# Rolling the PE and SP expert steps of a mixture-of-experts decoder layer into hardware loops

## The reference, cut to what matters

```python
logits = (x @ w_router + b_router).astype(jnp.float32)
top_logit, top_idx = lax.top_k(logits, TOP_K)            # TOP_K = 4 of N_EXPERTS = 32
top_w = jax.nn.softmax(top_logit, axis=-1)
...
def expert_block(args):
    xk, e = args
    a = xk @ w_up[e] + b_up[e]                           # D = 1024 -> 2 * 1024
    a_glu = jnp.minimum(a[:, :D_EXPERT], SWIGLU_LIMIT)
    a_lin = jnp.clip(a[:, D_EXPERT:], -SWIGLU_LIMIT, SWIGLU_LIMIT)
    o = a_glu * jax.nn.sigmoid(SWIGLU_ALPHA * a_glu) * (a_lin + 1)
    return o @ w_down[e] + b_down[e]                     # 1024 -> 1024
```

## Time and profile before

| | |
|---|---|
| median of three runs | 1538.55 us (1538.19 to 1539.16) |
| the profiled execution | 1538.55 us, span from first to last instruction 1536.5 us |
| PE busy | 1407.7 us (92% of the span), 9490 matmuls |
| DVE, ACT, POOL busy | 515.4, 272.5, 24.3 us |
| mean granted TensorE clock | 0.976 of full speed |
| read from HBM | 452.54 MB, 296 GB/s over the span |

### The profile page before, as it was taken

One profiled execution on the slowest core, in us unless ns is written; L12 is line 12 of the kernel. 1 busy time (PEld: TensorE's weight loads), 2 busy tenths in 40 slices (PEclk: granted clock), 3 DMA queues, 4 the chain that ended last, 5 costly groups with the idle time before them and its releaser, 6 DMA issues.

```text
span 1536.5 us, 23462 instructions
## 1 busy us (share of the span) xinstructions
PE 1407.7 (92%) x9490; PEld 859.0 (56%) x9490; DVE 515.4 (34%) x1339; ACT 272.5 (18%) x454; POOL 24.3 (2%) x43
## 2 busy tenths in 40 slices
PE   5699897799999999999999999999999999999996
PEld 4577675544455554545555555555555455555554
DVE  2279633311233322313332234333232232234333
ACT  1111201201121111101121211112221111211113
POOL 1021000000000000000000000000000000000000
PEclk9899998699999999999999999999999999999998
DMA  9933767146599995877999999999999689999930
GB/s 301 360 138 110 271 242 280 46 154 215 203 341 378 380 333 203 318 273 274 365 378 370 378 377 378 380 379 378 368 381 351 231 315 359 381 378 378 377 116 32
DMA packets 225543, 456.01 MB, mean 297 GB/s; under 512 B 4992, under 2 KB 5624, under 8 KB 225365
## 3 DMA queue, kind: packets, MB, share of 16 engines
q1 hardware_dynamic: 225050, 452.74, 81.2%
q0 software_dynamic: 160, 1.00, 0.2%
q10 hardware_dynamic: 203, 0.22, 0.0%
HBM read 452.54 MB, written 2.01 MB: 296 GB/s over the span
## 4 chain that ended last, share of the span: by engine, by line
PE 73%; ACT 5%; issue 3%; DVE 2%; DVEq 0%; ACTq 0%
PE ps L1138 51%; PE ps L1112 8%; PE ps L1192 7%; PE ps L1144 4%; ACT ufull L546 2%; ACT sq L528 1%; ACT sq L550 1%; PE ps L1223 1%; DVE uv L869 1%; PE ps L1093 1%; PE ps L1062 1%; PE ps L948 0%; PE ps L1259 0%; DVE hT L897 0%; PE ps L1070 0%
## 5 line engine op out<-in xcount | busy, mean ns | idle before, releaser
L1138 PE MATMUL ps<-ring,sq 128*64 128x256 f32 (+1 forms) x2848 | 398.3, 397 | 25.5 <-ACT sq L550 25.5
L1138 PEld LDWEIGHTS ps<-ring,sq 128*64 128x64 f32 (+1 forms) x2848 | 226.9, 141 | 177.7 <-issue 88.1
L843 DVE TENSOR_SCALAR sg<-ps 128x512 f32<-128x512 f32 x64 | 44.3, 692 | 538.9 <-PE ps L1144 538.9
L1138 PE MATMUL ps<-ring,ufull 128*64 128x256 f32 (+1 forms) x1408 | 198.5, 400 | 12.2 <-ACT ufull L546 12.2
L1138 PEld LDWEIGHTS ps<-ring,ufull 128*64 128x64 f32 (+1 forms) x1408 | 114.1, 142 | 90.0 <-issue 28.7
L542 ACT ACTIVATE pbuf<-sg 128x512 f32<-128x512 f32 x64 | 40.3, 630 | 558.3 <-DVE sg L843 558.3
L1112 PE MATMUL ps<-rows,ufull 128*64 128x256 f32 (+1 forms) x732 | 121.5, 412 | 5.2 <-issue 5.2
L846 DVE TENSOR_SCALAR wpool<-ps 128x512 f32<-128x512 f32 x64 | 44.3, 692 | 242.8 <-PE ps L1144 242.8
L1192 PE MATMUL ps<-ufull,sq 64*128 64x288 f32 (+1 forms) x528 | 122.6, 443 | 3.3 <-ACT sq L550 1.6
L986 PE MATMUL ps<-hT,ring 128*128 128x288 f32 x448 | 112.5, 413 | 10.9 <-DVE hT L643 9.2
L869 DVE TENSOR_TENSOR uv<-uv,ps 128x288 f32<-128x288 f32 x264 | 107.3, 451 | 19.7 <-PE ps L1192 12.4
(11 more groups left out here) (199 smaller groups left out, 968.0 us busy)
## 6 DMA issues: line engine op xcount, KB each, us to landing
ring<-in_w_up_dram SPq DMA_DIRECT2D x96, 2048.0 KB, 11.1
ring<-in_w_down_dram SPq DMA_DIRECT2D x48, 2048.0 KB, 10.7
pbuf<-in_w_up_dram SPq DMA_DIRECT2D x16, 2048.0 KB, 9.0
sg<-in_w_up_dram SPq DMA_DIRECT2D x16, 2048.0 KB, 11.4
ring<-in_w_ada_dram SPq DMA_DIRECT2D x12, 2048.0 KB, 10.4
pbuf<-in_w_down_dram SPq DMA_DIRECT2D x8, 2048.0 KB, 10.2
sg<-in_w_down_dram SPq DMA_DIRECT2D x8, 2048.0 KB, 11.7
ring<-in_w_in_dram SPq DMA_DIRECT2D x7, 2048.0 KB, 20.1
```

The lines of the kernel that those rows point to most:

```text
L843: V.tensor_scalar(glu, ps[:, UP_BANKS[2 * h], :], LIMIT, None, ALU.min)\
L1138: ins = pe.matmul(ps[a * width:(a + 1) * width, UP_BANKS[j], 0:cols], tokens(k), w[:, k, a * cols:(a + 1) * cols], start=(k == 0), stop=(k ...
```

## The change

Two Python loops over the eight groups of four experts become hardware loops: SP's in `expert_weights` and PE's in the pass that always runs. PE's stream then holds the code of four experts once, and at its end a branch back to its beginning; the step number is a register. So the values of the semaphore waits in it (`2 * n + 1`, `KT * g + 7`, `turn * 16 + ...`) are computed into registers by instructions of the engine's sequencer, the three token counts are loaded from an address that depends on a register (`bass.ds(e + i, 1)`), and SP's DMAs take a source address from a register. What is computed, the order of the work, the tiles and the waits stay.

```diff
             sp.wait_ge(m_ready, KT)
-            for step in range(NE // UNROLL):
+            with sp.Fori(0, NE // UNROLL) as step:
                 expert_weights(0, step)
...
                 sized(first, lambda width: (gather(width), turn_gathered(p * GAT, width)))
-                def four_experts(step):
+                with pe.Fori(0, NE // UNROLL) as step:
                     turn = p * (NE * EXPERT_CHUNKS // NRING) + step * TURNS
                     for u in range(UNROLL):
                         e = step * UNROLL + u
...
-                            last, this, nxt = (pe.value_load(cnti[0:1, e + i:e + i + 1],
+                            last, this, nxt = (pe.value_load(cnti[0:1, bass.ds(e + i, 1)],
                                                              min_val=0, max_val=NT) for i in range(3))
...
-                if fixed:
-                    with pe.Fori(0, NE // UNROLL) as step:
-                        four_experts(step)
-                else:
-                    for step in range(NE // UNROLL):
-                        four_experts(step)
                 pe.wait_ge(y_out, 2 * n0 + 2 * NE + 1)
```

## The result

The changed kernel takes 1618.21 us (median of four runs, 1611.12 to 1619.69) against 1538.86 us before: ratio 1.0487, 95% interval 1.0465 to 1.0510, slower by 79 us. The forecast was 1579 us, at most 1612. The sign was right, the size was half.

What follows compares the result with a forecast made beforehand. PE was taken to bound the kernel; register work 5.8, jump stalls 19.6 and slow clock 14.7 us made 40.1 us on top of 1538.55, so 1579 us, range 1546 to 1612.

Steps and rivals of the forecast that it cites:

- SP's loop is free: SP's weight stream: register work delays each DMA issue well under 1 us, covered by more than 20 us of slack; cost 0.
- The jump back has to fetch its target: PE, seven jumps back: 0.22 MB of code for four experts exceeds the 128 KiB held, so every jump misses.
- The size of the stall: PE at the seven jumps back: 2.8 us extra each, 19.6 us in all; ends 0 and 56 us.
- F = 4.9: Time in us to fetch code at a jump back, the middle of 1.9 and 8.0 us read in the mixer.
- c = 3: Cover in us: PE's sequencer's lead over PE at the end of `down`, taken from 0.9 to 7.15.
- The clock behind the jump: PE's first matmuls after each jump run at the lower clock: 2.1 us each, 14.7 us for seven.
- Register work: PE's wait values computed in registers: 0.18 us per expert, 5.8 us for 32; ends 0 and 18 us.
- The hidden jump: First rival: PE's jump is covered or its code kept, only register work left; 1544 us, up to 1560; chance 0.2.
- no change: Third rival: cover enough for everything on PE, additions at 0.05 us, 1.6 us in all; 1540 us; chance 0.06.
- faster: Rival: PE's gap behind each `y_out` shrinks because the loop's code stays in place; 11 us gained, 1527 us; chance 0.04.
- The second rival: PE's preamble outgrows a 0.9 us cover: 0.8 us at all 32 experts, jumps up to 5 us; 1620 us; chance 0.08.
- The fourth rival: PE's 0.40 us of issue behind each `y_out` is late code, not the branch; kept code gives 1527 us; chance 0.04.

Runs made afterwards that it cites:

- sp_loop: Only SP's loop made a hardware loop in the kernel before, PE's 32 experts left in a row: 1540.17 us, ratio 1.0003.
- wide_loop: The changed kernel's PE and SP loops of eight steps, with only the 128-column body of each piece: 2211.81 us, against 2212.54 us for the same bodies unrolled.
- ring6_loop: Both hardware loops with one expert per step (31 jumps back) and expert weights in six slots instead of eight: 1541.24 us, 1.0011 of the kernel before.
- quiet_loop: PE's loop alone, SP unrolled, weight chunk DMAs after the first two loading one row block of eight: 1577.63 us, 1.0253 of the kernel before.
- early_branch: The kernel before with the waits for hg_out, sel_ready and y_out moved inside the two bodies, behind PE's branch: 1534.05 us, ratio 0.9965.
- ring6_flat: The kernel before, PE and SP still unrolled, with expert weights in six slots instead of eight: 1539.83 us, ratio 0.9996.

## Why the prediction was wrong in size

- **PE bounds the kernel, SP's loop is free, DVE and ACT only shift.** Right: `sp_loop`, and in the kernel after no wait of PE for a landing in the expert stage.
- **The jump back has to fetch its target.** Right, and now shown. The trace: seven stretches at every fourth expert, and 142 packets. The runs: `wide_loop` and `ring6_loop`, whose bodies of some 77 and 55 KB are kept, pay nothing. The rule of the Trainium skill (Runtime: NRT & Kernel Launch, section Instruction fetch mechanics) puts PE's code memory at 128 KiB, and the limit in these runs lies between 77 KB and 0.22 MB, which agrees. The same section of the Trainium skill words its rule on branches for a window of two blocks of 16 KiB; for PE these runs speak against so small a window, since bodies of 55 and 77 KB were kept.
- **The size of the stall, the step that failed.** "With F = 4.9 and c = 3 ... the extra is 4.9 + 1.9 - 3.0 - 1.0 = 2.8 us, and seven are 19.6 us." Measured: 55.8 us, 8.0 each. That is the upper end that the text gave (8 us each, 56 us) and did not use; but that the two agree is luck. By the text's formula no gap could be longer than 8.0 + 1.9 - 0.9 = 9.0 us, and five of the seven are 10.27 to 11.14; the mean comes down to 9.0 by the two short ones. I took the middle of 1.9 and 8.0 us for the fetch and a cover of 3 out of 0.9 to 7.15, with no row behind either choice, and one fetch per jump. `quiet_loop` shows the first half of what the stall is: with the weight stream thinned the mean gap of the seven falls from 9.0 to 4.6 us, so about half the stall is the code packets standing among weight packets. The stretches of the earlier trace rows had that load too (376 GB/s from 172 to 181 us, 390 from 249.8 to 254), so their 1.9 to 8.0 us held it already, but could not say which end was the right one. The second half is open in part and follows behind this list.
- **The clock behind the jump.** Right in kind and nearly in size: 13.3 us instead of 14.7, at six of the seven jumps. The jump with 3.18 us of idleness kept its full clock (32 matmuls in 3.67 us), like the 1.91 us in the earlier trace rows; those of 7.12 us and more did not.
- **Register work.** 0.18 us per expert were taken, 0.09 came at line 546 and none at line 550: 3.7 us instead of 5.8.
- **The rivals.** The hidden jump, no change and faster are out. The second rival named a sum near the measured one (1620 us), by luck: it had 0.8 us at each of the 32 experts in it, and the 24 gaps within steps have not moved. The fourth rival's reading of the 0.40 us as late code is not what `early_branch` shows: moving the branch took 0.16 us of it, with the code streamed as before, and `ring6_loop`, with its code kept, still has 0.39.
- **The range.** It ended at 1612 because the stall's upper end was put together with little else. 56 us of stall, 14.7 of clock and 5.8 of registers, all from the text, are 76.5 us, 1615 us.

**The open half of the stall.** These are the timeline's lines at the jump ahead of expert 16, in the kernel after:

```profile
975.02 7.13 PE L1138 MATMUL ps<-ring,ufull 128*64 128x256 f32 x64 [0.63 <-ACT ufull L546]
992.43 1.12 PE L1138 MATMUL ps<-pbuf,sq 128*64 128x256 f32 x4 [10.28 <-issue]
```

`down` ended at 982.15. Two code packets move in the gap, at 983.9 and at 989.7 us, and PE starts 2.7 us behind the second; the next moves at 993.0. At expert 4 of `quiet_loop` the two move 3.2 us apart instead of 5.8, and PE starts 2.9 us behind the second. So a typical jump seems to wait for two fetches, one after the other.

What each brings is not shown: the first may be code behind the loop (the extra packets per jump would fit), or the second may be the block with the narrow body, which stands behind the wide one. The jump ahead of expert 8 speaks for the latter: there only one packet, at 673.2, moves between the end of `down` (671.56) and PE's start (678.67), and the wide body is the one that runs. The last 2.7 us need not be the register loads: in the mixer's stretches of the earlier trace rows, where no register is loaded, a code packet moves at 176.5 and at 249.1 us, and PE goes on at 178.79 and 251.76, 2.3 and 2.7 us later. No run separates these, nor how much of `down` is queued when the jump is reached. So the estimate of 3.6 us of cover from the 64 entries that the Trainium skill gives (TensorE: Matmul & The Clock Gate, section Architectural detail: the array is 16× 32×32, not 1× 128×128) is neither borne out nor refuted.

## What to carry to other kernels

Before a long unrolled body becomes a hardware loop, compare the body's code with what the engine keeps. The packets of the instruction queue per stretch give its size; here 55 and 77 KB were kept and 0.22 MB were not. Above that size the jump back waits for its code, here 10 us at a typical jump and 5 with an eighth of the weight stream, so a kernel whose DMA engines are full has the most to lose; the matrix engine also lost its full clock for some microseconds behind it. If a loop is wanted for its short code, shorten the step until it fits (here by dropping two weight slots) before asking anything else. Where a sequencer both waits and branches, let it branch first: here that gave 0.16 us each time.

## What was unexpected

- Code fetch competes with data: the same jump, ahead of expert 16, costs 10.3 us of idleness with weights at full rate and 5.3 with an eighth of them.
- 31 jumps back to code at hand, in `ring6_loop`, leave no gap over 1.05 us between experts on PE.
- A hardware loop of a single step leaves next to no trace in what runs (23466 instructions instead of 23462): it is no test for the cost of registers.
- Two weight slots of eight were not needed: `ring6_flat` runs at 0.9996 of the kernel before.
